# A two-layer decoder trunk in fp32: one token stream in three chunks, against two token halves that take turns on TensorE

## The chip, the cores and the metric

One core of a Trainium2 chip runs the whole program in one launch. The metric is the device time in microseconds. TensorE, VectorE (DVE), ScalarE (ACT), GpSimd (POOL) and SyncE (SP) each have a queue of their own, worked off in order, and wait for each other by semaphores.

## The reference

1024 prompt tokens and 8 x 4 sample tokens, width 1024, two layers, everything in fp32:

```
h = x
# layer 0: gated linear attention (4 heads, dk 128, dv 256), then ConvFFN
q, k, v, r, glr = split(rms(h) @ w_in)            # gates: log_sigmoid(glr @ w_gate_up + b) / 16
o   = chunked recurrence(q, k, v, gates, state)   # a state of 128 x 256 per head and sequence
h  += rms( (rms(o) * silu(r)) @ w_out )
h  += rms( conv_ffn(rms(h)) )
# layer 1: one shared K/V from h; sliding window (128) attention, 16 query heads, 2 kv heads
k, v = rms(h) @ w_kv ;  q = rms(h) @ w_q
h  += rms( softmax(q k + bias, with a sink per head) v @ w_o )
h  += rms( conv_ffn(rms(h)) )
# conv_ffn: u, val = x @ w_up (2816 each); c = causal conv of width 3 over tokens of u; (gelu(c) * val) @ w_down
```

Outputs are h, the states, the last two rows of u per layer, and the window of K and V.

## The kernel before

All activations are kept transposed: features on the 128 partitions, tokens along the free axis. The 1056 tokens are cut into three chunks of 352 columns (NC, CW). A large fp32 product is made of three products in fp32r: every operand is split into a rounded part and the rest (w_hi and w_lo, act_hi and act_lo), and lo x hi, hi x lo and hi x hi are added up in PSUM (project, L582, and down, L598).

Weights come as 190 blocks of 128 x 1024 in one fixed order. Each passes SP (DMA into w_raw, L538), ACT (w_hi, w_round, L543) and POOL (w_lo, w_rest, L547), in a ring of three slots, and is used for all 1056 tokens: 24 matmuls for each of three chunks. So a block holds TensorE for 72 matmuls.

The stages stand one behind the other: the boundary 0 (norm of x), the gated attention (a loop over 4 heads), boundary 1, ConvFFN (22 tiles of u and val, and after each second tile 24 units of down products, which DVE adds into acc, L606), boundary 2 with keys and values, the attention (a loop over 2 kv heads: projections of queries, then 32 iterations over blocks of 128 queries, then the down products), boundary 3, ConvFFN, boundary 4. At a boundary, for all tokens and chunk by chunk: ACT squares (L331), PE sums with a matrix of ones over the eight feature tiles (pe_sums, L488), ACT makes rstd (L337 and L339), DVE scales, adds the residual (L407, L414) and norms (L425), ACT rounds (L355), POOL takes the rest (L454).

In the attention loop (pe_attn) an iteration is two score matmuls (L1432), up to four transposes of the probabilities (L1449), up to four value matmuls (L1460), and one transpose of the output (L1468). No projection stands between them, except for query(11) in the first.

Order is set by the order in which the code is written; there is no scheduler.

## Time and profile before

| | |
|---|---|
| median of 3 runs | 2923.36 us (2915.23 to 2926.82) |
| profiled execution, span | 2931.7 us (no other time is given for it) |
| mean granted TensorE clock | 0.926 |
| TensorE busy | 93% |
| VectorE, ScalarE, GpSimd busy | 50%, 31%, 21% |
| instructions | 40564 |
| bytes moved | 144.20 MB |

A page of the profile gives busy time for each engine, slices of the span, the chain of waits and groups of instructions. A matmul's duration includes its way through the array, so that durations of matmuls overlap; what a matmul costs in a stream is read from the distance of starts. The granted clock is 1.00 at 2.4 GHz and 0.50 at 1.2 GHz.

### The profile page before, as it was taken

The page shows a single profiled execution, that of the slowest core. Times are in us where ns is not written, and L with a number is a line of the kernel's source. Part 1 is how long each engine was busy: PE and PEld are TensorE (multiplying, and loading weights), DVE is VectorE, ACT ScalarE, POOL GpSimd, SP SyncE. Part 2 cuts the span into 40 slices and gives each one's busy share as a digit, 9 for nine tenths or more (in the row PEclk, how much of TensorE's full clock was granted, in tenths as well). Part 3 has the DMA queues.
Part 4 walks back from the last instruction along what each step waited for, and adds up shares of the span by engine and source line. Part 5 has one row for each costly group of instructions (what it writes and reads, how often), then busy time and mean ns, then how long its engine had stood idle before and what let it go on. Part 6 is the DMA issues. An engine that isn't in the chain of part 4 may idle for free.

```text
span 2931.7 us, 40564 instructions
## 1 busy us (share of the span) xinstructions
PE 2738.1 (93%) x15861; PEld 2568.0 (88%) x15861; DVE 1458.9 (50%) x2222; ACT 911.5 (31%) x1449; POOL 619.8 (21%) x227
## 2 busy tenths in 40 slices
PE   6999989978999999999977999999799999999996
PEld 5988887966999999999966778877599999999996
DVE  3536363647544444444465464364554444444445
ACT  5332323235322222222253351352542222222223
POOL 3111110202422222222224100200242222222220
PEclk9989898989999999999988758957899999999998
DMA  7111111111111111111102200300111111111111
GB/s 164 39 53 41 51 38 45 51 38 60 63 49 43 43 43 43 50 50 43 51 41 94 68 1 15 90 1 1 74 61 44 50 43 43 43 43 43 51 42 62
DMA packets 44913, 144.20 MB, mean 49 GB/s; under 512 B 9407, under 2 KB 16772, under 8 KB 41860
## 3 DMA queue, kind: packets, MB, share of 16 engines
q1 hardware_dynamic: 43092, 134.00, 13.9%
q10 hardware_dynamic: 1728, 8.91, 0.8%
q8 instruction: 63, 1.03, 0.1%
q14 instruction: 30, 0.25, 0.0%
HBM read 124.74 MB, written 19.17 MB: 49 GB/s over the span
## 4 chain that ended last, share of the span: by engine, by line
issue 58%; PE 20%; POOL 10%; DVE 8%; ACT 3%; POOLq 0%; DMA 0%; SPq 0%; DVEq 0%; ACTq 0%
PE banks L582 8%; POOL w_lo L547 8%; PE banks L598 5%; DVE normed L425 2%; DVE acc L407 2%; PE banks L488 1%; DVE h_chunk L414 1%; PE banks L763 1%; PE banks L756 1%; PE banks L663 1%; POOL acc L477 1%; POOL o_lo L1653 1%; PE banks L709 1%; ACT L339 1%; DVE gat L980 0%
## 5 line engine op out<-in xcount | busy, mean ns | idle before, releaser
L582 PE MATMUL banks<-act_hi,w_lo 128*128 128x352 f32 x2952 | 968.4, 328 | 23.5 <-POOL act_lo L454 9.0
L582 PE MATMUL banks<-act_hi,w_hi 128*128 128x352 f32 x2952 | 956.2, 324 | 0.0
L582 PE MATMUL banks<-act_lo,w_hi 128*128 128x352 f32 x2952 | 955.5, 324 | 0.0
L547 POOL TENSOR_TENSOR w_lo<-w_raw,w_hi 128x1024 fp32r<-128x1024 f32 x190 | 493.6, 2606 | 1869.7 <-ACT w_hi L543 1869.7
L582 PEld LDWEIGHTS banks<-act_hi,w_lo 128*128 128x128 f32 x2952 | 561.5, 190 | 31.9 <-issue 13.1
L582 PEld LDWEIGHTS banks<-act_lo,w_hi 128*128 128x128 f32 x2952 | 563.0, 191 | 1.1
L582 PEld LDWEIGHTS banks<-act_hi,w_hi 128*128 128x128 f32 x2952 | 560.8, 190 | 0.0
L606 DVE TENSOR_TENSOR acc<-acc,banks 128x352 f32<-128x352 f32 x720 | 373.8, 521 | 353.5 <-PE banks L598 353.3
L543 ACT ACTIVATE w_hi<-w_raw 128x1024 fp32r<-128x1024 f32 x190 | 196.2, 1051 | 742.7 <-PE banks L598 586.7
L598 PE MATMUL banks<-h_hi,w_lo 128*128 128x352 f32 x1056 | 343.1, 325 | 9.6 <-issue 9.6
L598 PE MATMUL banks<-h_lo,w_hi 128*128 128x352 f32 x1056 | 343.5, 325 | 0.0
L598 PE MATMUL banks<-h_hi,w_hi 128*128 128x352 f32 x1056 | 342.8, 325 | 0.0
L1340 DVE SCALAR_TENSOR_TENSOR c<-u,par_tile,c 128x1072 f32<-128x1072 f32 x44 | 58.7, 1335 | 304.2 <-ACT c L1274 304.2
L598 PEld LDWEIGHTS banks<-h_hi,w_lo 128*128 128x128 f32 x1056 | 200.1, 189 | 10.4 <-issue 10.2
L598 PEld LDWEIGHTS banks<-h_lo,w_hi 128*128 128x128 f32 x1056 | 200.2, 190 | 0.2
L598 PEld LDWEIGHTS banks<-h_hi,w_hi 128*128 128x128 f32 x1056 | 200.1, 189 | 0.0
L1265 ACT ACTIVATE u<-banks 128x352 f32<-128x352 f32 x132 | 59.8, 456 | 334.9 <-PE banks L582 327.6
L1342 DVE SCALAR_TENSOR_TENSOR c<-u,par_tile,c 128x1072 f32<-128x1072 f32 x44 | 147.5, 3352 | 1.6
L1356 DVE TENSOR_TENSOR hf<-c,banks 128x352 f32<-128x352 f32 x132 | 70.2, 685 | 151.0 <-PE banks L582 104.3
L1366 DVE TENSOR_TENSOR h_lo<-hf,h_hi 128x1056 fp32r<-128x1056 f32 x44 | 94.4, 2146 | 88.5 <-ACT h_hi L1282 88.5
L488 PE MATMUL banks<-squares_pre,ones 128*128 128x352 f32 x192 | 80.2, 582 | 47.2 <-ACT squares_pre L331 47.2
L488 PEld LDWEIGHTS banks<-squares_pre,ones 128*128 128x128 f32 x192 | 45.0, 241 | 82.6 <-issue 61.7
(213 smaller groups left out, 3227.8 us busy)
## 6 DMA issues: line engine op xcount, KB each, us to landing
w_raw<-wall SPq DMA_DIRECT2D x190, 512.0 KB, 3.5
h_chunk<-xT SPq DMA_DIRECT2D x6, 1408.0 KB, 9.5
h_scratch<-h_chunk SPq DMA_DIRECT2D x3, 1408.0 KB, 4.7
h_chunk<-h_scratch SPq DMA_DIRECT2D x3, 1408.0 KB, 10.0
yT<-h_chunk SPq DMA_DIRECT2D x3, 1408.0 KB, 4.7
gstates<-state ACTq DMA_DIRECT2D x4, 1024.0 KB, 4.9
gla_s<-gstates ACTq DMA_DIRECT2D x4, 1024.0 KB, 3.9
bias_scratch<-bias_rows SPq DMA_DIRECT2D x1, 3064.0 KB, 43.6
```

Source lines behind the costliest of these rows:

```text
L407: last = nc.vector.scalar_tensor_tensor(ACC[:, c, n], ACC[:, c, n], col(g), RS[:, c], ALU.mult, ALU.mult)
L488: last = nc.tensor.matmul(PS[:, s["bank"], 0:CW], ones[:], squares(s)[:, n], start=(n == 0), stop=(n == KT - 1))
L543: nc.scalar.activation(WH[:, slot], WR[:, slot], ACT.Copy).then_inc(w_hi, 1)
L547: nc.gpsimd.tensor_tensor(WL[:, slot], WR[:, slot], WH[:, slot].bitcast(fp32), ALU.subtract).then_inc(w_lo, 1)
L582: last = nc.tensor.matmul(PS[:, bank, 0:CW], w, a[:, k, chunk(c)], start=(k == 0 and first), stop=(k == KT - 1 and w is wh and a is AH))
L598: last = nc.tensor.matmul(PS[:, 6 + m % 2, 0:CW], w, a[:, t, chunk(c)], start=(t == 0 and x == 0), stop=(t == 1 and x == 2))
L606: nc.vector.tensor_tensor(a, a, PS[:, 6 + m % 2, 0:CW], ALU.add).then_inc(dn_add, 1)
L1265: last = nc.scalar.activation(U[:, 2 + c * CW:2 + c * CW + n], PS[:, c, 0:n], ACT.Copy)
L1340: nc.vector.scalar_tensor_tensor(C[:, 0:CV], U[:, 1:1 + CV], PC[:, 17:18], C[:, 0:CV], ALU.mult, ALU.add).then_inc(cv1, 1)
L1342: nc.vector.scalar_tensor_tensor(C[:, 0:CV], U[:, 0:CV], PC[:, 16:17], C[:, 0:CV], ALU.mult, ALU.add).then_inc(cv2, 1)
L1356: last = nc.vector.tensor_tensor(HF[:, c * CW:c * CW + n], C[:, c * CW:c * CW + n], PS[:, 3 + c, 0:n], ALU.mult)
L1366: nc.vector.tensor_tensor(HL[:, t], HF[:], HH[:, t].bitcast(fp32), ALU.subtract).then_inc(hl, 1)
```

## The change

The tokens are cut in two halves: half 0 is prompt tokens 0 to 511, one chunk of 512 columns; half 1 is prompt tokens 512 to 1023 and the 32 sample tokens, two chunks of 272 columns. The order of the work is: the gated attention as eight turns (four heads of half 0, then four of half 1); ConvFFN of half 0, of half 1; attention of half 0, of half 1; ConvFFN of half 0, of half 1. Each half goes through its own stream of weights (366 blocks in place of 190, from the same array in memory). A list, weight_order, gives the order.

Residual and norms of one half (h, one tensor acc per half now, no longer loaded to its own tensor) are cut into nine steps, and each step is put into the queues of ACT, DVE, PE and POOL between the other half's work: at places of the turns (GLA_STEPS), at the ConvFFN's tiles 0 to 8, and at steps of the attention (ACT_AT, DVE_AT, PE_AT). Squares are folded on DVE (L489 to L497), and PE makes one sum per chunk (L503). The old residual is read back from DRAM through ACT's queue (L520, L525). For each half the causal convolution keeps the last two columns of half 0 in a tensor halo.

In the gated attention the recurrence of a head first makes all four state products of the half and then the outputs; the query and key projections of the next turn stand between the outputs. In the attention each of the 32 iterations per half is followed by half a projection or two (half 0) or four (half 1) down units. The probabilities are divided before they are transposed, and the value product has the values as weights, so the output is already transposed and the transpose L1468 is gone. All loops are written out.

```diff
 RL = 383
+HALF = ((0, 512), (512, 544))
+CHUNKS = (((0, 512),), ((0, 272), (272, 272)))
+RING, RAW = 3, 2
...
+def weight_order():
...
+        tile(0, 0)
+        tile(0, 1)
+        for g in range(1, FG):
+            tile(g, 0)
+            downs(g - 1)
...
+            tile(g, 1)
+        downs(FG - 1)
...
+    ffn(0)
+    ffn(1)
+    att(0)
+    att(1)
+    ffn(2)
+    ffn(3)
...
+        def w_load(sp, b):
+            if b >= RAW:
+                sp.wait_ge(w_lo, b - RAW + 1)
+            sp.dma_start(WR[:, b % RAW], wall[rows[b]]).then_inc(w_in[b % RAW], 16)
...
+        def round_after(act, name):
+
+            w_round(act, BLK[name] + RING)
...
-        def pe_sums(pe, s):
...
-                for n in range(half.start, half.stop):
-                    last = nc.tensor.matmul(PS[:, s["bank"], 0:CW], ones[:], squares(s)[:, n],
-                                            start=(n == 0), stop=(n == KT - 1))
+        def pe_sum(pe, i, kind, X, bank):
+            n = NORMS[i, kind, X]
+            pe.wait_ge(ps_done, 2 * n)
+            for c, (o, w_) in enumerate(CHUNKS[X]):
+                last = nc.tensor.matmul(PS[:, bank + c, 0:w_], ones[:], RS[X][:, o:o + w_], start=True, stop=True)
+            last.then_inc(ss_done, 1)
...
+        def dve_post(dve, i, X, m):
+            p = POSTS[i, X]
+            dve.wait_ge(rs_done, NORMS[i, "post", X])
+            for n in range(m * KH, m * KH + KH):
+                last = nc.vector.scalar_tensor_tensor(ACC[X][:, n], ACC[X][:, n], col(POST_G[i] + n), RS[X][:],
+                                                      ALU.mult, ALU.mult)
+            last.then_inc(po_done, 1)
+            dve.wait_ge(po_done, 2 * p - 1 + m)
+            dve.wait_ge(h_in, 32 * (2 * p - 1 + m))
+            nc.vector.tensor_tensor(ACC[X][:, part(m)], ACC[X][:, part(m)], NM[X][:], ALU.add).then_inc(ha_done, 1)
...
+        def act_step(act, i, X, step, bank):
+            if step in (0, 1):
+                act_square(act, i, "post", X, step)
+            elif step == 2:
+                act_rstd(act, i, "post", X, bank)
+                act_h_load(act, i, X, 0)
+            elif step == 3:
+                act_h_load(act, i, X, 1)
...
+                outgate(0, SECOND)
+                keys_by_token()
+                outgate(1, FIRST)
+                state_deltas()
+                outgate(1, SECOND)
...
+                    gates(u + 1)
...
+                    query(u + 1, FIRST)
+                outputs(0)
+                outputs(1)
+                if X:
+                    sample_outputs()
+                if more:
+                    query(u + 1, SECOND)
+                outputs(2)
+                outputs(3)
...
+                    key(u + 1, FIRST)
...
+                    key(u + 1, SECOND)
+                pe.wait_ge(gq_f, u + 1)
...
+            for s in range(NIT + 3 + X):
+                d, w = divmod(s, 8)
+                if s < NIT:
+                    scores(s)
+                if w < 2 and d < 4:
+                    query(X, 2 * d + 1, (FIRST, SECOND)[w])
+                elif w < 4 and d < 3:
+                    query(X, 2 * d + 2, (FIRST, SECOND)[w - 2])
...
+                if 2 <= s < NIT + 2:
+                    transposed(s - 2)
+                if w >= 4 and 1 <= d < 4:
+                    downs(d - 1, range((w - 4) * units, (w - 3) * units))
...
+                if 3 <= s < NIT + 3:
+                    values(s - 3)
...
+            for t in range(FT):
+                if 1 <= t <= (4 if f == 3 else 8):
+                    dve_step(dve, *FFN_PASS[f], t - 1)
...
+                conv(t)
+                product(t)
+                if t % 2 == 0 and t:
+                    adds(t // 2 - 1)
+                lo(t)
+            adds(FG - 1)
```

**TensorE in the attention.** One iteration before (kg and q are keys and queries, scores the probabilities, o_tok the output by token):

```order
L1432 MATMUL banks<-kg,q_109 128x256 [waits att_biased]
L1432 MATMUL banks<-kg,q_109 128x256
L1449 MATMUL banks<-ident,scores 128x128 [waits att_pt_copied,att_exp]
L1449 MATMUL banks<-ident,scores 128x128
L1460 MATMUL banks<-vg,probs_t 128x64 [waits att_o_scaled,att_pt_copied]
L1460 MATMUL banks<-vg,probs_t 128x64 x3
L1468 MATMUL banks<-ident,o_tok 128x128 [waits att_hi,att_o_scaled]
```

And an iteration of half 0 in the changed kernel, in a step with down products (o_hi and o_lo are the attention's outputs):

```order
L1466 MATMUL banks<-kg,q_101 128x256 [waits att_biased]
L1466 MATMUL banks<-kg,q_101 128x256
L1479 MATMUL banks<-ident,probs 128x128 [waits att_pt_copied,att_scaled]
L1479 MATMUL banks<-ident,probs 128x128 x3
L445 MATMUL banks<-o_hi,w_lo 128x512 [waits down_added,w_lo_done]
L445 MATMUL banks<-o_lo,w_hi 128x512
L445 MATMUL banks<-o_hi,w_hi 128x512
...
L445 MATMUL banks<-o_hi,w_hi 128x512
L1494 MATMUL banks<-probs_t,v_tok 64x128 [waits att_lo,att_pt_copied]
L1494 MATMUL banks<-probs_t,v_tok 64x128 x3
```

Twelve large matmuls of 512 columns have moved between the transposes and the values of every iteration.

**VectorE, residual and norms.** Before, at boundary 1, behind the last down products' adds and with nothing else around:

```order
L606 TENSOR_TENSOR acc<-acc,banks 128x352 [waits down_full] x24
L407 SCALAR_TENSOR_TENSOR acc<-acc,gain_cols,rstd 128x352 [waits rstd_done]
L407 SCALAR_TENSOR_TENSOR acc<-acc,gain_cols,rstd 128x352 x3
L414 TENSOR_TENSOR h_chunk<-h_chunk,acc 128x1408 [waits post_norm_done,h_in0]
L407 SCALAR_TENSOR_TENSOR acc<-acc,gain_cols,rstd 128x352 x4
L414 TENSOR_TENSOR h_chunk<-h_chunk,acc 128x1408 [waits post_norm_done]
```

In the changed kernel the same work of half 1 (acc_54, with the residual in normed_56) stands between two iterations of half 0's attention:

```order
L1651 TENSOR_REDUCE stats<-scores 128x2 [waits att_sink,att_biased]
L1653 TENSOR_SCALAR stats<-stats 128x2 [waits att_max]
L1659 RECIPROCAL stats<-stats 128x2 [waits att_exp]
L1661 TENSOR_TENSOR probs<-probs,stats 128x2x128 [waits att_rden]
L535 SCALAR_TENSOR_TENSOR acc_54<-acc_54,gain_cols,rstd_58 128x544 [waits rstd_done]
L535 SCALAR_TENSOR_TENSOR acc_54<-acc_54,gain_cols,rstd_58 128x544 x3
L540 TENSOR_TENSOR acc_54<-acc_54,normed_56 128x2176 [waits h_in,post_norm_done]
L1646 TENSOR_TENSOR scores<-banks,bias 128x2x256 [waits att_exp,att_scores]
L1651 TENSOR_REDUCE stats<-scores 128x2 [waits att_sink,att_biased]
```

What is behind L540 in the queue, the bias and the maximum of the next scores, now stands behind its wait for h_in, a DMA.

## Rows read from the trace of the kernel before

**Rows 1.** Page, busy shares and granted clock in 40 slices.
```profile
PE 2738.1 (93%) x15861; PEld 2568.0 (88%) x15861; DVE 1458.9 (50%) x2222; ACT 911.5 (31%) x1449; POOL 619.8 (21%) x227
PEclk9989898989999999999988758957899999999998
```

**Rows 2.** Stretches: length, busy us and instructions by engine, clock, DMA share, GB/s.
```profile
61.00:219.00 158.00, 151.42 (x873) 140.32 (x874) 71.99 (x66) 58.23 (x84) 33.82 (x11) 0.91 0.14 50
...
546.00:730.00 184.00, 154.31 (x807) 131.31 (x808) 109.09 (x138) 78.69 (x93) 29.94 (x10) 0.91 0.14 51
730.00:1497.00 767.00, 762.18 (x4743) 760.54 (x4742) 364.01 (x517) 187.21 (x232) 184.94 (x68) 1.00 0.13 46
1497.00:1590.00 93.00, 63.03 (x270) 48.41 (x268) 75.67 (x86) 55.75 (x57) 39.70 (x12) 0.84 0.18 70
...
1656.00:1806.00 150.00, 142.55 (x695) 114.78 (x695) 85.91 (x252) 62.38 (x225) 9.44 (x4) 0.65 0.01 4
1806.00:1901.00 95.00, 84.37 (x515) 79.80 (x515) 31.79 (x56) 20.31 (x46) 21.20 (x9) 0.95 0.27 75
...
2052.00:2130.00 78.00, 58.90 (x233) 44.66 (x234) 46.08 (x67) 40.80 (x39) 21.37 (x7) 0.87 0.17 69
...
2896.00:2932.00 36.00, 17.45 (x70) 12.05 (x68) 23.81 (x34) 12.21 (x13) 0.00 (x0) 0.83 0.29 120
```

**Rows 3.** TensorE in order of time: start, duration, instruction; two clocks.
```profile
55.58 0.49 PE L582 MATMUL banks<-act_lo,w_hi 128*128 128x352 f32 x1
55.87 0.49 PE L582 MATMUL banks<-act_hi,w_hi 128*128 128x352 f32 x1
...
63.50 0.32 PE L582 MATMUL banks<-act_hi,w_hi 128*128 128x352 f32 x1
63.65 0.32 PE L582 MATMUL banks<-act_hi,w_lo 128*128 128x352 f32 x1
```

**Rows 4.** Weight loads in order of time, small fp32 products at full clock.
```profile
319.50 0.52 PEld L756 LDWEIGHTS banks<-gqt,gstates 128*128 128x128 f32 x4
```

**Rows 5.** TensorE in order of time, score matmuls of two successive iterations.
```profile
1703.26 1.23 PE L1432 MATMUL banks<-kg,q 64*128 64x256 f32 x4
...
1707.28 1.23 PE L1432 MATMUL banks<-kg,q 64*128 64x256 f32 x4
```

**Rows 6.** Groups by line and form: busy us, mean ns | idle before, releaser.
```profile
L606 DVE TENSOR_TENSOR acc<-acc,banks 128x352 f32<-128x352 f32 x720 | 373.8, 521 | 353.5 <-PE banks L598 353.3
L1342 DVE SCALAR_TENSOR_TENSOR c<-u,par_tile,c 128x1072 f32<-128x1072 f32 x44 | 147.5, 3352 | 1.6
L1340 DVE SCALAR_TENSOR_TENSOR c<-u,par_tile,c 128x1072 f32<-128x1072 f32 x44 | 58.7, 1335 | 304.2 <-ACT c L1274 304.2
L1565 DVE TENSOR_TENSOR scores<-banks,bias 128x512 f32<-128x512 f32 x56 | 38.2, 682 | 3.0 <-PE banks L1432 3.0
...
L543 ACT ACTIVATE w_hi<-w_raw 128x1024 fp32r<-128x1024 f32 x190 | 196.2, 1051 | 742.7 <-PE banks L598 586.7 <-PE banks L582 151.6 <-DMA w_raw<-wall 4.5
L337 ACT ACT_TABLE_LOAD x24 | 30.8, 1283 | 0.4
...
L547 POOL TENSOR_TENSOR w_lo<-w_raw,w_hi 128x1024 fp32r<-128x1024 f32 x190 | 493.6, 2606 | 1869.7 <-ACT w_hi L543 1869.7
```

**Rows 7.** Waits of TensorE: us in total, times, longest.
```profile
PE banks L488 <- ACT squares_pre L331: 47.2, 14, 6.5
PE banks L736 <- DVE gat L980: 17.3, 4, 4.4
```

**Rows 8.** DMA issues: KB each, median us to landing.
```profile
w_raw<-wall SPq DMA_DIRECT2D x190, 512.0 KB, 3.5
...
h_chunk<-h_scratch SPq DMA_DIRECT2D x3, 1408.0 KB, 10.0
```

**Rows 9.** VectorE and GpSimd in order of time, in a tile of the ConvFFN.
```profile
1046.13 3.36 DVE L1342 SCALAR_TENSOR_TENSOR c<-u,par_tile,c 128x1072 f32<-128x1072 f32 x1
...
1045.75 2.60 POOL L547 TENSOR_TENSOR w_lo<-w_raw,w_hi 128x1024 fp32r<-128x1024 f32 x1 [7.59 <-ACT w_hi L543]
```

2949 lines of the change are left out of this document (1564 added, 1385 removed), and 3 rows, old and new, of the table POOL_LO.

## The prediction

> **What bounds the kernel now.** I read the busy shares, then a table by stage, then the matmuls one by one, then what the other engines pay per instruction. TensorE is busy for 93% of the span, but its granted clock is not full everywhere [rows 1]. The table by stage tells where [rows 2]. The two ConvFFNs (730 to 1497, and one like it from 2130 to 2896) are 767 and 766 us at clock 1.00, with 762 us of TensorE busy: nothing is left there but matmuls. Everything else is 1399 us: 730 us up to the first ConvFFN, 633 us from 1497 to 2130 (the boundary, keys and values, the attention and a boundary again), 36 us of tail. In it are two stretches of 93 and 78 us where the residual and the norms run for all tokens at once (TensorE busy 63 and 59 us, mostly with sums of squares), and two of 150 us in which the attention iterates with nothing beside it, at clock 0.65. So the reader should see a kernel with two perfect stages and 1399 us in which latency and a low clock cost something.
>
> **The price of a large matmul.** With 352 columns, starts lie 0.29 us apart at 1.2 GHz and 0.16 us at 2.4 GHz (55.58 to 55.87; 63.50 to 63.65, 0.159 over longer runs) [rows 3]; 4743 of them in 762 us are 0.161 each [rows 2]. There are 13,176 before (counted from the code: 8856 in projections, 4320 in down products). After, there are 4392 of 512 columns and 8784 of 272: the same number of matmuls, the same number of columns (4,637,952), so whether the price goes by the column, by the instruction or by a mix of both, a triple 512+272+272 costs what three of 352 cost, 0.48 us. I take that; by the column it is 0.233 and 0.124 us. The exception is a floor per instruction above 0.124 us. The small fp32 products show one for their weight loads: four in 0.52 us, the last lasting about 0.19 like those of the large products, are 0.11 us apart [rows 4]. 0.124 is just above 0.11. If the 0.160 were itself a floor at full clock, 272 columns would cost 0.160 too and 512 columns 512/2.4 GHz = 0.213: the price then is 8784 x 0.160 + 4392 x 0.213 - 13,176 x 0.160 = +233 us. The bounds are 0 and +233, value taken 0, because the row that is nearest (the same kind of weight load, rows 4) has its floor at 0.11.
> The Trainium skill (TensorE: Matmul & The Clock Gate, Back-to-back issue gap) says that in a stream of weight load and matmul pairs the spacing is set by both operations, and gives N/2.4 + 2.5 ns for the matmul alone. By the formula 352 columns are 149 ns; the trace has 160 and disagrees, so something beside the columns is paid, which is what keeps the floor alive as a rival.
>
> **Sums of squares and boundaries.** Of 192 matmuls with ones 24 remain (one per 512 or 272 columns, after VectorE has folded the eight tiles), and with them the wait of TensorE for ScalarE's squares, 47.2 us [rows 7]. Up to the first ConvFFN this frees what stood between the last down product of the gated attention and the ConvFFN, 36 us of the stretch 546 to 730. What hides it: one half's residual and norms run while TensorE works on the other half.
>
> **Gated attention, now 730 us to the ConvFFN.** Four heads become eight half-turns. Start: only half of x is needed first, and TensorE is in steady work about 15 us sooner (-15). Boundary: -36. The serial chain behind the last output of a head is now run eight times: ScalarE copy, square, silu, log, exp and round, with three table loads of 1.28 us, weight roundings of 1.05 us between (ScalarE costs 1.05 us per 1024 columns, a VectorE pass of two operands 1.34 per 1072) [rows 6]. For 512 tokens that is: copies 1.8, square 1.05, silu 2.3, key copy and roundings 2.6, log 1.9, exp 1.9, three VectorE passes 2.5, ScalarE rounding 1.05, the rest 1.2 = 16 us. TensorE has beside it half a query projection 2.8, outputs 0.9, a key projection 5.6, sum 0.9 = 10. So 6 to 8 us idle per half-turn, less in the second half, where the samples fill. The wait for the decayed keys (4.3 us per head, 17.3 in all, now named as gat) [rows 7] comes eight times too. Before, each head pays about 12 us for both; now 8 x 12 - 4 x 12 = +48. Queries and keys of the next turn stand between the state products, where the clock now is low (0.91 over a head, 61 to 219): -25. One half's norms in the turns of the other, with a wait for a DMA in VectorE's queue: +15. Sum: 730 - 15 - 36 + 48 - 25 + 15 = 717. The doubtful term is +48: bounds 0 (if the chain hides) and +110 (16 us bare, eight times, less before).
>
> **Attention and its boundaries, now 633 us.** At 1.2 GHz an iteration takes 4.02 us (1703.26 to 1707.28) and TensorE is what it waits for [rows 5]. If that is all clock, at 2.4 GHz it is 2.0 us. In the new order half a projection or two to four down units stand in each step: 12 x 0.233 = 2.8 us (half 0) or 24 x 0.124 = 3.0 (half 1), which should also keep the clock up. Steps: 36 x 4.8 = 173 us, and 37 x 5.6 = 207 us (with 0.6 for the samples). Uncovered: the first query 5.6 us, the last downs 48 x 0.233 = 11.2 and 96 x 0.124 = 11.9. Sum 409 us, keys and values of both halves partly in the ConvFFN before (6 us there). VectorE per step: three passes of 512 columns at 0.68, three small ones at 0.2, 0.2 for the low part = 2.9, in half of the steps two adds of 0.69 (0.15 + 512/0.96 GHz, by L606 and L1565) [rows 6], and once in a while a norm step of 2 to 5 us: 4.3 on average, just under TensorE. So it costs where a norm step falls: four residual steps, each of which waits in VectorE's queue for a DMA that ScalarE issues only after the rstd. A read of 1408 KB took 10 us, three queued [rows 8]; 1 MB alone I take as 5.5 us. Behind that wait are the scores' bias and maximum, so exp, transposes and values, and the adds that free the down banks: 4 x 6 = 24, and 12 for the rest. Attention: 445 us, -188. Bounds: 409, and 633 if nothing is won.
>
> **ConvFFN, now 1533 us.** The matmuls stay 2 x 760. Each block of weights is now loaded, rounded and split twice: 366 blocks for 190. In half 0 a block feeds 24 matmuls of 0.233 = 5.6 us. It costs a DMA of 3.5 us [rows 8], 1.05 us of ScalarE and 2.6 us of GpSimd [rows 6]: no queue is full (GpSimd 2.6 of 5.6), but the ring has three slots. After a pair of down blocks one block is ready (5.6 us of work), the next is rounded from then on: 0.1 + 1.05 + 2.6 = 3.8 us. It just fits; cover left 1.8 us. Before, the same wait had 11.5 us of cover. It fails where GpSimd does a low half of the activations first (2048 columns, 5 us): once or twice per ConvFFN half, 2 us each. The residual steps hold VectorE about 8 us (four passes 2.7, the DMA, 2.2): the convolution, the product and the adds are behind it, and TensorE has banks for one tile: about 3 us each. Per half 4 + 6 = 10 us: 1520 + 40 = 1560 us, +27. Bounds: +5 and +120.
>
> **Tail**, now 36 us [rows 2]: half the tokens, but from the start, since the last sum needs all down products, and the residual comes by DMA in two parts, one behind the other: 39 us.
>
> **Sum**, against the profiled execution: 717 + 445 + 1560 + 39 = 2761 us for 2931.7. No time of that execution is given beside its span; the median of the runs is 2923.36, 0.3% under it. In the median's measure: 2752 us.
>
> **Rivals.** (A) Waits hide better: chain +10 in place of +48, attention 410, ConvFFN +5: 2752 - 38 - 35 - 22 = about 2655. For it: VectorE is at 50%, ScalarE at 31%. Against: both queues are in order. 0.13.
> (B) VectorE and GpSimd hold each other up. The same instruction over the same columns costs 1335 ns (L1340) and 3352 ns (L1342) [rows 6], and GpSimd's w_lo starts just before the second (1045.75 and 1046.13) [rows 9]: 2.0 us lost. With 366 splits it hits more. In the gated attention some 25 two-operand passes per half-turn, GpSimd busy a quarter of it, 1.3 us each: 8 us x 8 = 64; attention 64 scalings: 20. 2752 + 84 = 2836. The Trainium skill (SBUF - State Buffer, Who interferes with whom) says of a VectorE instruction with two SBUF inputs and a GpSimd one that reads SBUF that the second to issue "fully blocks". The trace agrees in L1342. I put 0.15 here: the clashes are there already, and only those on a chain cost.
> (C) The floor: matmuls of 272 columns start 0.160 us apart. Place: all of half 1. Price +233: 2752 + 233 = 2985, slower than before. It decides when 8784 x (f - 0.124), less the 4392 x 0.020 that 512 columns then save, is more than 171: from f = 0.153 us on. Against: rows 4. For: nothing in the trace has an fp32r matmul other than 352 columns, and 0.160 is unexplained. 0.10.
> (D) The interleaving doesn't raise the clock: steps of 4.0 us and a projection at 1.2 GHz, 5.1 us, make 9.1 x 73 = 664 + 40 for the ends, which with 717 + 1560 + 39 is 3020, about 3010 by the median. Against: the stretch from 1806 to 1901, down products and queries, has 0.95 [rows 2]. 0.04.
>
> **Numbers.** Forecast 0.58, A 0.13, B 0.15, C 0.10, D 0.04. The forecast's own range is 2700 to 2805; 2640 to 2930 leaves out C, D and a bit of A. This kernel's runs lie 0.4% apart, so 0.5% is what can be told from no change: that is 2909 to 2938. Faster by more: the first three but for an ill mix, 0.81. Slower: C and D, and some of B with a dearer ConvFFN, 0.14. Within: 0.05.
>
> **What would show it.** Start distances of 0.233 and 0.124 us in the ConvFFNs at clock 1.00; ConvFFN halves of about 390 us; clock over 0.9 in the attention and about 440 us for it; w_lo as a releaser of TensorE for under 40 us; the normed and rounded outputs (go_lo) as releaser of its down products for 50 us. Wrong would be: 0.160 us at 272 columns; TensorE idle at w_lo after each pair of downs; VectorE over 80% in the attention.

## The result and the profile after

The changed kernel takes 3051.68 us (median of 4 runs, 3042.43 to 3054.61), the kernel before 2925.09 beside it: ratio 1.0428, interval 1.0387 to 1.0469. The forecast was 2752 us, faster; the kernel is slower by 127 us.

The page of the changed kernel: busy us, share, instructions, and the granted clock in 40 slices.
```profile
PE 2610.9 (86%) x15437; PEld 2280.8 (75%) x15437; DVE 1700.0 (56%) x2493; ACT 1089.3 (36%) x1664; POOL 990.5 (32%) x388
...
PEclk8888887788799999999999888888899999999997
```
TensorE fell from 93 to 86% busy [rows 1], GpSimd rose from 620 us of busy time to 990. The clock is higher where the attention iterates and lower at the start.

The stretches of the changed kernel (columns as in [rows 2]): gated attention, two ConvFFN halves, attention, two ConvFFN halves, tail.
```profile
0.00:849.50 849.50, 621.98 (x3385) 540.98 (x3386) 376.35 (x580) 297.77 (x402) 182.45 (x75) 0.84 0.23 68
849.50:1702.20 852.70, 808.50 (x4841) 727.12 (x4840) 501.12 (x661) 301.37 (x396) 367.72 (x142) 0.98 0.30 96
1702.20:2204.50 502.30, 393.79 (x2448) 303.18 (x2449) 337.61 (x598) 203.31 (x486) 105.15 (x38) 0.85 0.21 67
2204.50:3017.30 812.80, 784.44 (x4763) 708.38 (x4761) 469.19 (x639) 278.90 (x375) 335.14 (x133) 0.98 0.30 95
3017.30:3051.40 34.10, 2.18 (x4) 1.18 (x4) 15.70 (x16) 7.97 (x6) 0.00 (x0) 0.54 0.40 131
```
Against the sum of the prediction: gated attention 849.5 for 717 (730 before), ConvFFN 1665.5 for 1560 (1533 before), attention 502.3 for 445 (633 before), tail 34.1 for 39. Only the attention won anything, 131 of the 188 us hoped for. In the ConvFFNs TensorE is no longer busy throughout, where it was before [rows 2].

TensorE of the changed kernel in order of time, both widths at full clock.
```profile
1105.32 0.40 PE L445 MATMUL banks<-h_hi,w_hi 128*128 128x512 f32 x1
1105.56 0.40 PE L445 MATMUL banks<-h_hi,w_lo 128*128 128x512 f32 x1
...
1500.04 0.29 PE L445 MATMUL banks<-h_hi,w_lo 128*128 128x272 f32 x1
1500.16 0.29 PE L445 MATMUL banks<-h_lo,w_hi 128*128 128x272 f32 x1
```
Over the long unbroken runs starts lie 0.2329 us apart with 512 columns and 0.1256 with 272. A triple (one matmul of 512 columns and two of 272) costs 0.4841 us and not 0.480: 4392 x 0.0041 = 18 us. There is no floor at 0.16; rival C falls.

The longest waits of TensorE in the changed kernel's gated attention, 0 to 849.5 us, and below them those of the kernel before, 0 to 730 us (us in total, times, longest).
```profile
PE banks L445 <- issue: 73.5, 8, 10.0
PE banks L715 <- DVE gkt L970: 35.2, 8, 4.6
PE banks L696 <- DVE gkt L897: 31.6, 12, 10.4
PE banks L425 <- DVE act_lo L563: 30.6, 2, 20.7
PE banks L503 <- DVE rstd L497: 14.9, 1, 14.9
...
PE banks L696 <- DVE gkt L892: 5.3, 1, 5.3
```
```profile
PE banks L582 <- POOL act_lo L454: 9.0, 2, 6.9
...
PE banks L598 <- DVE go_lo_end L941: 7.9, 1, 7.9
...
PE banks L663 <- DVE gkt L863: 3.3, 4, 0.8
...
PE banks L598 <- DVE go_lo L922: 1.7, 3, 0.6
```
Four waits grew: at the output's down products (L445, in wait for go_lo) 73.5 us for 9.6, at the keys by token (L715) 35.2 for 17.3 [rows 7], at the level scores (L696) 36.9 for 3.3, at the start 30.6 for 9.0. Together 137 us, and idle time is what the stage grew by: 227.5 us of TensorE not busy (849.5 - 622.0) for 87.8. (At the start the idle time took the place of sums of squares; the steady work begins no later than before.)

What stands before one of the eight: TensorE, VectorE and ScalarE of the changed kernel in order of time.
```profile
238.87 1.12 PE L821 MATMUL banks<-gsq,ones 128*128 128x512 f32 x2 [2.53 <-DVE gsq L1005]
249.05 0.76 PE L445 MATMUL banks<-go_hi,w_lo 128*128 128x512 f32 x1 [9.05 <-issue]
...
243.92 1.42 DVE L1008 SCALAR_TENSOR_TENSOR go<-go,gain_cols,grs 128x512 f32<-128x512 f32 x2 [5.11 <-ACT grs L1177]
245.37 1.23 DVE L1012 TENSOR_TENSOR go<-go,gr 128x1024 f32<-128x1024 f32 x1
...
247.72 1.23 DVE L1016 TENSOR_TENSOR go_lo<-go,go_hi 128x1024 fp32r<-128x1024 f32 x1 [0.52 <-ACT go_hi L1186]
...
239.97 1.28 ACT L1175 ACT_TABLE_LOAD   x1
241.26 0.69 ACT L1175 ACTIVATE grs<-banks,eps_col 128x512 f32<-128x512 f32 x1
241.97 1.28 ACT L1177 ACT_TABLE_LOAD   x1
243.26 0.63 ACT L1177 ACTIVATE grs<-grs 128x512 f32<-128x512 f32 x1
```
TensorE sums the squares at 238.87, go_lo is done at 248.95, the down products start at 249.05, and TensorE has nothing in between. The releaser reads "issue", since the profile's own match (w_lo) had come long before; the end of L1016 is what it waited for. In the kernel before, the same place behind a head's sum of squares (L717) is filled with a projection:
```profile
350.09 1.35 PE L717 MATMUL banks<-gsq,ones 128*128 128x352 f32 x4
351.01 0.59 PE L582 MATMUL banks<-act_hi,w_lo 128*128 128x352 f32 x1
...
367.29 0.40 PE L598 MATMUL banks<-go_hi,w_lo 128*128 128x352 f32 x1 [0.58 <-DVE go_lo L922]
```

VectorE by line and form, changed kernel: busy us, mean ns.
```profile
L1323 DVE TENSOR_TENSOR h_lo<-hf,h_hi 128x512 fp32r<-128x512 f32 x44 | 90.0, 2046 | 56.2 <-ACT h_hi L1384 56.2
...
L1292 DVE SCALAR_TENSOR_TENSOR c<-u,par,c 128x512 f32<-128x512 f32 x44 | 87.0, 1978 | 115.1 <-ACT c L1374 115.1
...
L535 DVE SCALAR_TENSOR_TENSOR acc<-acc,gain_cols,rstd 128x512 f32<-128x512 f32 x32 | 34.7, 1145 | 4.8 <-ACT rstd L511 4.8
```
And in order of time, with GpSimd's split (first and third row) and VectorE beside it (second and fourth).
```profile
1039.44 2.40 POOL L411 TENSOR_TENSOR w_lo<-w_raw,w_hi 128x1024 fp32r<-128x1024 f32 x1 [3.03 <-ACT w_hi L407]
...
1040.02 0.69 DVE L457 TENSOR_TENSOR acc<-acc,banks 128x512 f32<-128x512 f32 x1 [0.29 <-PE banks L445]
...
1056.76 2.40 POOL L411 TENSOR_TENSOR w_lo<-w_raw,w_hi 128x1024 fp32r<-128x1024 f32 x1 [1.89 <-ACT w_hi L407]
...
1057.42 2.29 DVE L1292 SCALAR_TENSOR_TENSOR c<-u,par,c 128x512 f32<-128x512 f32 x1 [4.82 <-ACT c L1374]
```
A pass with both operands in SBUF that comes during a split (1057.42) takes 2.29 us and ends 0.55 us behind it (1059.16); a sum whose second operand lies in PSUM (1040.02) takes 0.69 us in the middle of one (so do all 24 of 512 columns that start in a split). In [rows 9] the reader saw the first; it is now the rule, for L1292 takes 1978 ns on average, where 812 is its price with GpSimd's instruction cut short (e4, below).

### The profile page after: what moved, and what is told of

The parts are those of the page before. It is cut to its first block, busy times and chain, and to the rows that moved or that the text cites. A ratio compares the mean times of both kernels' runs of the same rounds, so it can differ in the third digit from the quotient of the medians.

```text
span 3051.4 us, 37488 instructions
## 1 busy us (share of the span) xinstructions
PE 2610.9 (86%) x15437; PEld 2280.8 (75%) x15437; DVE 1700.0 (56%) x2493; ACT 1089.3 (36%) x1664; POOL 990.5 (32%) x388
## 4 chain that ended last, share of the span: by engine, by line
PE 64%; DVE 14%; ACT 8%; issue 7%; DMA 3%; POOL 3%; SPq 1%; ACTq 0%; DVEq 0%
PE banks L425 34%; PE banks L445 23%; ACT w_hi L407 3%; POOL w_lo L411 2%; DMA w_raw<-wall 2%; DVE normed L550 2%; PE banks L696 1%; DVE c L1292 1%; DMA normed<-h_scratch 1%; DVE acc L535 1%; DVE stats L1651 1%; DVE scores L1646 1%; DVE normed L489 1%; PE banks L752 1%; POOL act_lo L563 1%
## 5 line engine op out<-in xcount | busy, mean ns | idle before, releaser
L411 POOL TENSOR_TENSOR w_lo<-w_raw,w_hi 128x1024 fp32r<-128x1024 f32 x366 | 903.9, 2477 | 1947.3 <-ACT w_hi L407 1947.1
L425 PE MATMUL banks<-act_hi,w_lo 128*128 128x272 f32 (+1 forms) x2952 | 993.5, 337 | 48.5 <-DVE act_lo L563 30.6
L425 PE MATMUL banks<-act_lo,w_hi 128*128 128x272 f32 (+1 forms) x2952 | 977.5, 331 | 0.0
L425 PE MATMUL banks<-act_hi,w_hi 128*128 128x272 f32 (+1 forms) x2952 | 977.0, 331 | 0.0
L407 ACT ACTIVATE w_hi<-w_raw 128x1024 fp32r<-128x1024 f32 x366 | 379.8, 1053 | 643.6 <-PE banks L445 580.7
L457 DVE TENSOR_TENSOR acc<-acc,banks 128x272 f32<-128x272 f32 (+1 forms) x624 | 322.7, 521 | 307.4 <-PE banks L445 307.4
L445 PE MATMUL banks<-h_hi,w_lo 128*128 128x272 f32 (+1 forms) x1056 | 362.0, 343 | 71.1 <-DVE acc L457 44.5
L445 PE MATMUL banks<-h_lo,w_hi 128*128 128x272 f32 (+1 forms) x1056 | 351.8, 333 | 0.0
L445 PE MATMUL banks<-h_hi,w_hi 128*128 128x272 f32 (+1 forms) x1056 | 351.2, 333 | 0.0
L1292 DVE SCALAR_TENSOR_TENSOR c<-u,par,c 128x512 f32<-128x512 f32 (+1 forms) x88 | 174.4, 1982 | 228.1 <-ACT c L1374 228.1
L445 PEld LDWEIGHTS banks<-h_hi,w_lo 128*128 128x128 f32 x1056 | 205.9, 195 | 96.1 <-DVE acc L457 49.0
L1323 DVE TENSOR_TENSOR h_lo<-hf,h_hi 128x512 fp32r<-128x512 f32 (+1 forms) x88 | 177.0, 2011 | 116.8 <-ACT h_hi L1384 116.8
L445 PEld LDWEIGHTS banks<-h_lo,w_hi 128*128 128x128 f32 x1056 | 207.4, 196 | 16.8
L445 PEld LDWEIGHTS banks<-h_hi,w_hi 128*128 128x128 f32 x1056 | 206.1, 195 | 16.5
L445 PE MATMUL banks<-go_hi,w_lo 128*128 128x272 f32 (+1 forms) x192 | 75.6, 394 | 85.7 <-issue 73.5
L445 PEld LDWEIGHTS banks<-go_hi,w_lo 128*128 128x128 f32 x192 | 45.2, 235 | 96.2 <-issue 79.1
```

Of the source, the lines that this page charges most:

```text
L407: nc.scalar.activation(WH[:, b % RING], WR[:, b % RAW], ACT.Copy).then_inc(w_hi, 1)
L411: nc.gpsimd.tensor_tensor(WL[:, b % RING], WR[:, b % RAW], WH[:, b % RING].bitcast(fp32), ALU.subtract).then_inc(w_lo, 1)
L425: last = nc.tensor.matmul(PS[:, bank, 0:n], w, a[X][:, k, o:o + n], start=(k == 0 and first), stop=(k == KT - 1 and w is wh and a is AH))
L445: last = nc.tensor.matmul(PS[:, bank, 0:w_], w, a[t][:, o:o + w_], start=(t == 0 and x == 0), stop=(t == 1 and x == 2))
L457: nc.vector.tensor_tensor(a, a, PS[:, bank, 0:w_], ALU.add).then_inc(dn_add, 1)
L1292: nc.vector.scalar_tensor_tensor(C[:, 0:cv], U[:, 1:1 + cv], PAR[:, t, 17:18], C[:, 0:cv], ALU.mult, ALU.add).then_inc(cv1, 1)
```

## The experiments

Times are medians; "before" ran beside each on the same chip (medians of 2917.7 to 2923.1 us; the changed kernel's own runs stood beside 2925.1, so differences to it are no surer than some 5 us). e4, e5, e6, e8, e10 and e15 leave out a part of the computation: they show what it costs, and are no kernels to use. The table gives the stages of each kernel's profiled execution, cut as above: behind the last down product of the gated attention, at the first scores of the attention, behind its last down product, behind the last of all.

```
                           median   gated    ConvFFN  atten-  ConvFFN  tail
                                    attn.    0, 1     tion    2, 3
the changed kernel         3051.7   849.5    852.7    502.3   812.8    34.1
e1  cover the norm         3047.3   844.8    852.5    502.5   814.4    34.2
e2  residual read early    3041.5   853.3    847.0    501.1   811.0    34.1
e3  bias rows in pieces    3037.4   837.7    850.5    501.1   811.0    34.1
e4  split of 128 columns   2914.7   800.5    815.5    470.2   789.5    34.4
e5  the same + idle work   3004.1   833.3    840.5    485.8   807.3    34.1
e7  FFN splits on VectorE  3064.9   849.8    849.0    502.5   825.2    35.1
e8  no log, no exp         3033.2   835.6    850.2    502.1   814.4    34.2
e9  split in four          3011.6   828.2    843.7    489.2   812.2    34.5
e10 narrow norm passes     2916.0   811.2    819.1    467.0   789.1    24.5
e14 e2 + e3 + e9           2988.5   811.2    840.7    488.7   808.7    33.6
e15 e4 + e10               2830.7   776.7    802.5    442.6   781.7    23.6
```

### e1, e8: the chain behind a head's output

```diff
-  pe.wait_ge(w_lo, BLK["o", u, 1] + 1)
+  if more: next_value(u + 1)      # value projection 0, FIRST, ahead of the downs
+  pe.wait_ge(w_lo, BLK["o", u, 1] + 1)
```


> Edit: in the gated attention the first half of the next half-turn's first value projection (12 matmuls of 512 columns, 2.8 us, or 24 of 272, 3.0 us) stands between the sum of squares of a head's output and the output's down products, where TensorE sat idle 8 to 10 us in each of the eight half-turns. Theory A (the chain log, exp, three passes, two roundings behind the sum is bare and its length is fixed): seven of the eight waits shrink by 2.8 to 3.0 us, the whole by 20 us, 3032 us. Rival (the wait is moved: behind the down products the next scores come before VectorE has their decayed factors): within 5 us of 3052.

Measured 3047.3, 4 us less. The waits of TensorE in its gated attention:
```profile
PE banks L702 <- DVE gkt L906: 42.4, 13, 12.0
...
PE banks L445 <- issue: 23.4, 8, 8.1
PE banks L425 <- POOL w_lo L411: 17.5, 7, 3.3
```
50 of the 73.5 us at the down products are gone, and the time isn't: 17.5 us turned up in front of the value block that wasn't split yet, and others at the level scores (L702 is L696 of the changed kernel). The rival was right, the wait moved.

```diff
-  activation(RS0, banks(X, 2), ACT.Ln, ...)   activation(RS0, RS0, ACT.Exp, scale=-0.5)
+  activation(RS0, banks(X, 2), ACT.Copy, ...)  activation(RS0, RS0, ACT.Copy, scale=0.5)
```


> Edit: in the norm of each head's output in the gated attention the logarithm and the exponential of ScalarE are plain copies (the inverse root is left out), so two table loads of 1.28 us and no more leave the chain behind the sum. e1 covered 2.8 us of that wait with work and gained only 4 us. Theory C (a half-turn is bound by its chain of dependent steps from the first scores to the last sum, 75 us or more whatever TensorE does meanwhile): each of eight half-turns is 2.6 us shorter, 3052 - 20 = 3032. Rival (e1 gained nothing because TensorE's own work bounds the half-turn): TensorE's idle time shrinks as in e1 and the time stays within 6 us of 3052.

3033.2, 18.5 us less, of 20 expected; the waits at the down products fell from 73.5 to 58.9 us. So what bounds a half-turn is the length of its chain: two copies in place of log and exp shortened the chain and with it the time, and 2.8 us of work put beside it did not.

### e2, e3: a late read, and small packets at the start

```diff
   elif step == 2:
+      act_h_load(act, i, X, 0)
       act_rstd(act, i, "post", X, bank)
-      act_h_load(act, i, X, 0)
```


> Edit: ScalarE issues the first read of the residual before it waits for the sum of squares, not behind the two activations that make rstd; the read starts about 4 us earlier in all eight residual steps. The prediction's step (VectorE's queue waits for this DMA and TensorE behind it, 3 us in each of four ConvFFN halves, 6 in each attention step): 3052 - 25 = 3027. Theory A (the first ConvFFN's waits show the DMA landing 1.0 us after VectorE's four passes, so only the passes themselves delay anything): 3052 - 5 at the tail and some more = 3043 to 3050, and the idle times of TensorE of 5 to 7.5 us in the ConvFFN stay.

3041.5: 10 us less (the runs of the two kernels overlap by a hair, 3042.43 against 3048.72, so 10 is near what can be told). The tail did not shorten. Theory A holds: of the prediction's four residual steps in the attention, "each of which waits in VectorE's queue for a DMA", none waits for it in the changed kernel's trace, and the four in the ConvFFNs wait 0.4 to 1.7 us each.
```diff
-  sp.dma_start(r_dram (16 heads), RB.broadcast)   # ahead of the gated attention
+  if 8 <= b < 24: sp.dma_start(r_dram[b - 8], RB[b - 8].broadcast)   # behind weight load b
```


> Edit: the bias rows (3064 KB written in rows of 1532 bytes, 36.6 us on the DMA engines at the start) lie in another buffer and are written head by head, one piece of 192 KB behind each of sixteen weight loads of the first turns. Theory A (that write fills the DMA engines at 97 GB/s from 23 to 50 us, and the third weight block waits behind it, so TensorE idles 20.7 us before its first query): the first query starts at about 38 us instead of 58, the whole is 18 to 20 us shorter, 3033 us. Rival (the pieces delay later weight blocks by 2.3 us each while the first turns are bound by latency anyway): 3045 to 3060.

3037.4: 14 us less. The wait before the first queries fell from 20.7 to 3.4 us; 11.8 us show in the stage. Here went the prediction's "-15" at the start: the same write stood in the kernel before, and the third weight block waits behind it (steady work begins at 58.3 us, for 63.1 before). Moving it in the kernel before gained nothing, however (e11, below).

### e4, e5, e9: what GpSimd's split costs, and how

```diff
-  gpsimd.tensor_tensor(WL[:, s], WR[:, r], WH[:, s], subtract)             # 1024 columns
+  gpsimd.tensor_tensor(WL[:, s, 0:128], WR[:, r, 0:128], WH[:, s, 0:128], subtract)   # b >= 3
```


> Edit: GpSimd makes only 128 of the 1024 columns of each low half of the weights from the fourth block on (the other columns keep old values: part of the split is left out), so its instruction shrinks from 2.5 to about 0.4 us, and with it both the latency of the ring and the time in which VectorE's passes are held. Theory B (VectorE is held up: the first convolution pass 2.3 us instead of 0.74, the four residual passes 4.9 instead of 2.7, and its queue stops TensorE): the stops of TensorE in the four ConvFFN halves (76 us) fall to about 25, with less time at the low clock; 3052 - 50 to - 80 = 2970 to 3000. Rival (the stops come from the norm passes and the order of VectorE's queue, not from the lock, and the low halves were ready in time): 3035 to 3050.

2914.7: 137 us less, twice what was expected, and level with the kernel before (0.9973, 0.9943 to 1.0004). VectorE by line and form in e4 (L1293 is L1292, L1324 L1323, L536 L535):
```profile
L1293 DVE SCALAR_TENSOR_TENSOR c<-u,par,c 128x512 f32<-128x512 f32 x44 | 35.7, 812 | 161.8 <-ACT c L1375 161.8
...
L1324 DVE TENSOR_TENSOR h_lo<-hf,h_hi 128x512 fp32r<-128x512 f32 x44 | 30.5, 692 | 56.9 <-ACT h_hi L1385 56.9
...
L536 DVE SCALAR_TENSOR_TENSOR acc<-acc,gain_cols,rstd 128x512 f32<-128x512 f32 x32 | 22.9, 777 | 6.4 <-ACT rstd L512 6.4
```
The same passes take 812 for 1978 ns and 692 for 2046. But the low halves were ready 2 us earlier too.
```diff
   gpsimd.tensor_tensor(WL[:, s, 0:128], ...).then_inc(w_lo, 1)
+  for n in (4, 3): gpsimd.tensor_tensor(IDLE[:, 0:n], ones.broadcast, ident.broadcast, subtract)
```


> Edit: as e4_short_split (128 of 1024 columns of each low half, the rest of the split left out), but behind the signal GpSimd makes two subtractions of 512 and 384 columns into a tile that nobody reads, so it is as busy as in the changed kernel while the low half is ready early. Theory B (VectorE is held up by a busy GpSimd, and that is what the 137 us of e4 were): the convolution pass stays at about 2.3 us, the whole at 3030 to 3055. Theory R (the 2.1 us that the low half came earlier were the gain, in the ring of three slots): 2915 to 2940. By a half of each: about 2985.

3004.1, between the theories and nearer to B: 89 of the 137 us come back with GpSimd's work although the low half is early, 48 don't. The split isn't clean, and not clean in both directions. The idle work is in two shorter instructions, so that the convolution pass is at 1.5 to 1.6 us, not 1.98; but GpSimd is busy for 3.06 us a block, where it was 2.48. So VectorE's part is about 89 us, not exactly. A rival, that the idle work holds up the next split in GpSimd's queue, does not show: TensorE's waits for w_lo are 23.2 us in the changed kernel, 12.2 in e4 and 4.8 in e5.
```diff
+  for x in range(0, 1024, 256): gpsimd.tensor_tensor(WL[:, s, x:x+256], ..., subtract)
```


> Edit: GpSimd splits each weight block in four subtractions of 256 columns in place of one of 1024, in the changed kernel; nothing is left out. By the durations measured (0.49 us for 128 columns, 1.36 for 512, 2.43 for 1024) a piece takes 0.77 us, a block 3.1 instead of 2.5. Theory B (VectorE's pass waits until the GpSimd instruction in its way has ended): it waits 0.77 us at most instead of 2.4, the convolution pass falls from a mean of 1.98 to about 1.2 us, and against 0.6 us more of latency of the ring (e4 less e5: 48 us for 2 us of it) the whole is at 3052 - 50 + 15 = about 3015. Rival (each of four pieces holds VectorE up once, so the sum is the same): 3052 to 3075.

3011.6: 40 us less with nothing left out, as theory B had it (3015). The convolution pass fell from 1978 to 1340 ns: VectorE is held for the length of the GpSimd instruction in its way. A block's split takes 3.4 us now for 2.5, and TensorE's waits for w_lo rose from 23.2 to 37.0 us.

### e7: the splits on VectorE

```diff
   conv(t);  + dve_rest(dve, ("u", f, t))
   product(t);  + dve_rest(dve, ("val", f, t))      (+ two behind the sums of the downs)
```


> Edit: in the four ConvFFN halves VectorE splits the weights (the same subtraction, at the place in its queue where ScalarE has just rounded the block), GpSimd elsewhere. Nothing is left out. Theory B (the lock is what costs, VectorE has time): a split on VectorE takes about 1.2 us, 264 of them 320 us, but 88 convolution passes fall from 2.0 to 0.8 us and 88 roundings from 2.0 to 0.75, 216 us back, and the residual passes by half; the ConvFFN stages fall from 852.7 and 812.8 us towards those of e4 (815.5 and 789.5): 3052 - 45 = 3007. Rival (VectorE's queue becomes the bound of a tile: 18 us per two blocks of work, its order delays the sums): slower than 3052, 3070 to 3100.

3064.9, 13 us more, with runs (3046.9 to 3072.9) that overlap those of the changed kernel: the 45 us of theory B did not come, and the rival's 3070 is not quite reached. The waits of TensorE from 850 to 3026 us:
```profile
PE banks L454 <- DVE w_lo L420: 51.3, 10, 8.8
PE banks L454 <- DVE acc L466: 31.5, 35, 2.2
```
The passes are short again (L1301 has a median of 0.80 us), but a low half now waits behind whatever stands in VectorE's queue, up to 8.8 us. Freeing VectorE from GpSimd's hold and losing GpSimd's own queue came to nothing.

### e10, e15: what the norms cost, and what is left

```diff
-  scalar_tensor_tensor(ACC[X][:, n], ACC[X][:, n], gain, RS[X][:], mult, mult)
+  scalar_tensor_tensor(ACC[X][:, n, 0:64], ACC[X][:, n, 0:64], gain, RS[X][:, 0:64], mult, mult)
   (squares, folds, residual sums and norm passes likewise, from the second norm on)
```


> Edit: after the first norm of x, every square, fold, residual pass and norm pass of a half works on 64 of its 512 or 544 columns (the rest of the residual and the norms is left out); all steps, their order, DMAs and waits stay. Theory N (the norm steps in VectorE's queue are what stops TensorE for 5 to 7.5 us a time in the ConvFFNs): the stops there fall from 77.6 us to the 20 to 25 that the ends of the halves and the ring cost, 50 us with the low clock behind them, attention 20 us, the gated attention's last half-turns 10: 3052 - 80 = 2972. Rival (the time of the passes hardly matters, it is the waits between engines and GpSimd's lock): 3052 - 25.

2916.0, 136 us less, far more than either theory: 38 in the gated attention, 57 in the ConvFFNs, 35 in the attention, 10 in the tail. So the half whose norms "run while TensorE works on the other half" pays for most of them: 136 us of time for 166 us less of VectorE's busy time (ScalarE's squares became shorter too, by 43 us, and were not separated). In the changed kernel a residual step holds VectorE for 8 us, 7.2 of them passes (rows of ConvFFN 1):
```profile
1301.99 4.88 DVE L535 SCALAR_TENSOR_TENSOR acc<-acc,gain_cols,rstd 128x512 f32<-128x512 f32 x4 [2.42 <-ACT rstd L511]
1307.91 2.29 DVE L540 TENSOR_TENSOR acc<-acc,normed 128x2048 f32<-128x2048 f32 x1 [1.03 <-DMA normed<-h_scratch]
```
The tile's convolution, product and sums stand behind it in the queue, and TensorE stopped for 7.5 us from 1322 us on, behind the second such step.


> Edit: the changed kernel with the short split of e4 and the narrow norm passes of e10 (both parts of the computation left out). Theory S (two separate costs, both on VectorE's chains): 3052 - 136 - 137 = 2779. Theory O (one cost seen twice, norm passes are long because GpSimd holds them up): 2870 to 2900. By the widths: of e10's 136 us about 54 were passes lengthened by the lock, so I take 2820. In either case the gated attention stays above 730 us, since its half-turns are bound by a chain of dependent steps that neither edit shortens much; under 720 would contradict that.

2830.7: 221 us of the 273 that e4 and e10 are worth alone, so they are two costs with an overlap of 52. The stretches of e15:
```profile
0.00:776.70 776.70, 596.84 (x3385) 520.14 (x3386) 304.89 (x580) 291.37 (x402) 57.74 (x75) 0.87 0.25 75
776.70:1579.20 802.50, 793.87 (x4841) 717.32 (x4840) 298.02 (x661) 289.19 (x395) 91.65 (x142) 1.00 0.32 102
1579.20:2021.90 442.70, 369.88 (x2448) 286.71 (x2449) 256.17 (x598) 191.06 (x486) 45.56 (x38) 0.92 0.24 75
2021.90:2803.60 781.70, 775.47 (x4763) 702.72 (x4761) 292.29 (x639) 269.84 (x375) 70.56 (x133) 1.00 0.31 99
```
Without both costs the attention takes 442.7 us, the ConvFFN 1584 and the gated attention 777, where the forecast had 445, 1560 and 717. That flatters the forecast, since these sums hold 36, 40 and 15 us for the norm steps and the ring, and e15 has taken most of that away. Against 409, 1520 and 702 the stages of e15 are 34, 64 and 75 us too long, and of the 64 the price of the matmuls is 13 (some 3170 triples by 0.0041).

### e6, e11, e12, e13, e16: the same cure for the kernel before

```diff
   # the kernel before, e6
-  gpsimd.tensor_tensor(WL[:, slot], WR[:, slot], WH[:, slot], subtract)
+  gpsimd.tensor_tensor(WL[:, slot, 0:128], WR[:, slot, 0:128], WH[:, slot, 0:128], subtract)
```


> Edit: the kernel before, with GpSimd making only 128 of the 1024 columns of each low half (part of the split left out). It has 190 splits instead of 366. If GpSimd's splits cost in proportion to their number (e4: 137 us for 366, 0.37 each), it gains 70 us: 2852. If its ConvFFN stays at 767 us (TensorE never stops there in the profile) and only the gated attention and the attention have the chains on which VectorE's passes lie, it gains 15 to 35 us: 2890 to 2910, and the change would be worth nothing even without the splits. If it gains nothing: 2925.

2867.6 beside 2923.1 (0.9799, 0.9764 to 0.9834), between the two expectations: the splits cost the kernel before 55 us, so the doubled number costs the change 137 - 55 = 82 more. Even without them it is 47 us behind (2914.7 for 2867.6).

The two gains don't lie in the same places. The attention from its first scores to its last down product, in the kernel before, in e6 and in e13 (below), columns as in [rows 2]:
```profile
1629.20:2080.40 451.20, 421.49 (x2224) 357.84 (x2220) 229.82 (x606) 155.74 (x519) 49.49 (x21) 0.74 0.11 35
```
```profile
1611.00:2021.70 410.70, 384.94 (x2224) 326.13 (x2220) 220.40 (x606) 155.47 (x519) 24.89 (x21) 0.83 0.12 38
```
```profile
1624.00:2029.50 405.50, 370.19 (x2224) 314.76 (x2220) 221.84 (x606) 156.16 (x519) 55.07 (x60) 0.86 0.12 38
```
Of the 59 us between the profiled executions of the kernel before and e6, 40 lie in this stage, 9 in the gated attention, 10 up to the first scores and 1 in the second ConvFFN. And it is TensorE's busy time that falls, with the clock at 0.83 for 0.74, not its idle time (30 us, then 26). Why the clock was granted higher with a shorter split, of which the stage has a dozen, no run shows. In the changed kernel e4 won 49 us in the gated attention, 60 in the ConvFFNs and 32 in the attention.

```diff
   # the kernel before, e11; e12 is e11 with e13's edit
-  sp.dma_start(r_dram, RB.broadcast)        # ahead of sp_gla
+  act.dma_start(r_dram, RB.broadcast)       # ahead of act_ffn(act, 0)
```


> Edit: in the kernel before, the bias rows lie behind the gated attention's tiles and are written by one DMA that ScalarE issues in front of the first ConvFFN, so the constants and weights of the gated attention don't wait for 43.6 us of small packets. Expected: TensorE waits 7 us there before the third part of the gate's projection, and the constants arrive at 57 to 60 us; the first head starts 8 to 12 us earlier, the ConvFFN hides the write: 2923 - 10 = 2913. Rival (the write takes the weights' bandwidth in the ConvFFN, a block lands too late): 2925 to 2940.

2938.0, ratio 1.0076 (1.0035 to 1.0117): slower by 0.8%, the rival. The write took 34.5 us in the ConvFFN, and TensorE stopped once, 11.9 us. The gain expected at the start is missing: the gated attention ends at 693 us, for 690 before.

> Edit: as e11, and GpSimd's split in four pieces of 256 columns, in the kernel before. By e6 a split without its columns is worth 55 us there. Theory B: a third to a half of that comes back where VectorE's passes are on chains, 15 to 25 us on top of e11: 2890 to 2900. Rival (four pieces hold VectorE up as often as one long one, and the split is 0.6 us longer): e11 or 5 us more.

2906.3, ratio 0.9926 (0.9893 to 0.996): 32 us below e11, more than the 15 to 25 expected, though 6 us above the time given. The pieces were the good half.

```diff
   # the kernel before, e13 (e16: steps of 128)
-  gpsimd.tensor_tensor(WL[:, slot], WR[:, slot], WH[:, slot], subtract)
+  for x in range(0, 1024, 256): gpsimd.tensor_tensor(WL[:, slot, x:x+256], ..., subtract)
```


> Edit: the kernel before with GpSimd's split in four pieces of 256 columns, nothing else. e12 (with the late rows, which alone cost 20 us against the runs of its own time) was 32 us below e11. Theory B (shorter instructions in the way of VectorE): 2918 - 25 to 32 = 2886 to 2893. Rival (e11's loss was peculiar to the late rows with long splits, so the two don't add): 2900 to 2915.

> Edit: as e13, in eight pieces of 128 columns, each 0.49 us, a block 3.9 us. If what matters is the longest wait of a VectorE pass (0.49 instead of 0.77), it is 3 to 8 us better than e13. If each piece costs VectorE a turn, or the ring a later block (3.9 instead of 3.1 us, with 11.5 us of work beside it), equal or up to 10 us worse.

e13: 2880.6 beside 2918.8, ratio 0.9886 (0.9843 to 0.9929), 5 us better than expected and the best kernel of the study with nothing left out, by one statement changed against the kernel before. e16: 2895.0, 0.9932 (0.9907 to 0.9957), 14 us behind e13, where 8 better to 10 worse was expected; the intervals overlap, so four or eight pieces can't be told apart. The pass that took 3352 ns on average [rows 6], in e13 and in e16:
```profile
L1344 DVE SCALAR_TENSOR_TENSOR c<-u,par_tile,c 128x1072 f32<-128x1072 f32 x44 | 74.6, 1694 | 1.6
```
```profile
L1344 DVE SCALAR_TENSOR_TENSOR c<-u,par_tile,c 128x1072 f32<-128x1072 f32 x44 | 62.4, 1417 | 1.6
```
VectorE is held for less, as in the changed kernel; but this pass stands in the ConvFFN, and the ConvFFN gained nothing by it (the second, with its boundary, took 823 us before and 822 in e13). 46 of the 52 us between the two profiled executions lie in the attention, in the stretches shown above, and there TensorE was busy for 51 us less at the clock of 0.86 and idle for 35 us in place of 30. So the gain of e13 is shown, and that it comes from shorter holds is not.

> Edit: the changed kernel with the early residual read of e2, the bias rows in pieces of e3 and the split in four of e9; nothing left out. If the three gains (10, 14 and 40 us) add: 2988. If they overlap in the gated attention, whose half-turns are bound by one chain: 2995 to 3005. In both cases still slower than the kernel before.

2988.5: the three gains add up, as far as the runs can tell. With all that costs nothing the changed kernel stays 2.6% behind (1.0259, 1.0221 to 1.0298).

## Why the prediction was wrong

**What bounds the kernel now.** Right, and the trap: the two ConvFFNs were perfect, so every change there could only lose. Shown: 1533 us became 1665.5.

**The price of a large matmul.** Right to 0.004 us a triple; +18 us, which the value 0 left out.

**Gated attention, +48 for the chain and the keys.** This is the step that failed first. It took "about 12 us for both" as what each head paid before. The rows of before have 17.3 us for the keys in four heads and 9.6 in all for go_lo, which is 6.7 a head: a head behind whose sum of squares a further projection stood (15.7 us of it, 351.0 to 366.7 in the trace of before) paid almost nothing for its norm. A half-turn has the same chain, and behind its sum nothing: the 5.6 us of key projection that the prediction counted as cover stand ahead of the sum, beside the first part of the chain only (230.5 to 236.3 in the trace of the changed kernel). The 12 us for a half-turn were nearly right (13.6 by the waits); the price before was not. By the waits the term is +64 for the norm's tail, +18 for the keys and +34 for the level scores, which had no term at all: 116 for 48. The bound of +110 was near, but only one of three waits had been thought of. The clock, -25, went the other way: the large matmuls of the stage lost some 60 us to stretches at 1.2 GHz against 16 before (start to start, less 0.2329, 0.1256 or 0.160 us each), and the stage's mean is 0.84 for 0.92. The start was -5, not -15. (These overlap with each other and with the norms and the splits below, so they don't add up to the 132 us.)

**Norms behind the other half.** The terms were +15, +36 and some 24 in the ConvFFNs: 75. e10 measures 136: 38, 35, 57 and 10 in the tail. In the ConvFFN and the gated attention VectorE's queue, not its load, is what TensorE stands behind. The reason given (the DMA in VectorE's queue) was wrong, as e2 shows. The hold of about 8 us was right in its length and wrong in what it is made of: 7.2 us of passes (four in 4.88 us where 2.7 were taken, the rest being GpSimd's hold, and 2.29) and 1.0 of DMA. What it does to TensorE was mis-sized, at 3 us a step in the ConvFFN. The attention's 36 was met by luck: 24 of it were for DMA waits that the trace doesn't have.

**ConvFFN, the ring.** The forecast charged 16 us for the ring of three slots in both ConvFFNs. Of the 60 us that e4 wins there, e5 keeps 18 (12.2 and 5.5), with the low half early and GpSimd busy: the latency costs about what was charged, and the other 42 us, by e5, are VectorE held up, which had no term. The doubled loads are a rival that no run took away: ScalarE waits 62.4 us for weights in 44 waits (22.4 at the start), for 4.5 in one before. What TensorE can feel of it in the ConvFFNs and the attention is within its 23.2 us at w_lo.

**Rival B** was the missing term: 82 us for the doubled splits by e4 and e6, where B had 84. That the sums agree is luck: B had 64 in the gated attention, 20 in the attention and nothing in the ConvFFN, and the differences of e4 and e6 by stage are 40, -8 and some 50. It was put at 0.15 since "the clashes are there already", though the change doubled them. Forecast and rivals were also taken one at a time: B and a dearer chain came together. The Trainium skill (SBUF - State Buffer, Summary: rules for kernel authors) has the rule that of a VectorE instruction with two SBUF inputs and a GpSimd one that reads SBUF the second to issue "fully blocks" until the first is done; the rows at 1056.76 and 1057.42 and the fall from 1978 to 812 ns in e4 agree, and so does e9.

**Attention.** Right in its mechanism: the clock is 0.85 over the stage, where in the kernel before two stretches of 150 us, in which the attention iterates, ran at 0.65 [rows 2]. The size was not: 502 for 445, and 34 us over the bare 409 even without splits and norms. Rival D named a time near the measured one (3010), for a reason that the clock refutes.

Left open: how the last 75 us of the gated attention in e15 divide between its doubled chain, the clock and the start; what the last 51 of the ConvFFN and 34 of the attention are; how much of e4's gain is latency alone, since a kernel with a late low half and an idle GpSimd was not tried; and why the kernel before is granted a higher clock in its attention with shorter splits.

## What to carry to other kernels

Halving a tile to overlap two streams halves the work beside each dependent chain and leaves the chain as long: count each wait of the old trace with what hid it, and take that cover away before pricing the new one. Work moved "behind the other half" still stands in an in-order queue, and whoever feeds TensorE stands behind it. If GpSimd runs beside VectorE, try shorter instructions on it: four pieces in place of one made the new kernel 1.3% faster, for 0.9 us more of latency a block, and the old one 1.1%, there by a higher clock in another place than the holds. The low halves of the activations, 4.7 to 4.9 us each on average and the longest instructions of GpSimd in the changed kernel, stayed whole in every run here.
